# A decode stage with a fourth place for value slices and two buffers for split weights

## What is computed

```python
p = x @ w_in                                    # (560 tokens, 2048) x (2048, 6664)
qa, ka, va, ... = jnp.split(p, ...)
...
k_past = cache_k[l][page_table].reshape(bs, past, H_ATT, HEAD_DIM)
v_past = cache_v[l][page_table].reshape(bs, past, H_ATT, HEAD_DIM)
z = einsum('bqhd,bkhd->bhqk', q, k) * SB_SCALE + bias
log_keep = where(mask, log_sigmoid(-z), 0)
log_pass = cumsum(log_keep, reverse=True) - log_keep
a = where(mask, exp(log_sigmoid(z) + log_pass), 0)
h_att = einsum('bhqk,bkhd->bqhd', a, v)
```

## Time and profile before

| | us |
|---|---|
| median of 3 runs (2784.31 to 2788.75) | 2785.24 |
| the profiled execution's own time | 2780.29 |
| its span in the profile | 2778.6 |
| first stage, from 0 to about | 966 |
| TensorE busy over the span | 2686.6 (97%) |
| DMA moved over the span | 691.84 MB |

### The profile page before, as it was taken

The page is one execution under the profiler, slowest core; times in us unless marked ns, Lnnn a source line. Parts: engine busy times, 40 slices in busy tenths (PEclk is TensorE's granted clock), DMA queues, the critical chain, the costliest instruction groups (busy, mean ns, idle before and its releaser), DMA issues.

```text
span 2778.6 us, 58915 instructions
## 1 busy us (share of the span) xinstructions
PE 2686.6 (97%) x25059; PEld 2545.9 (92%) x25059; DVE 1931.2 (70%) x2366; ACT 1096.1 (39%) x1615; POOL 340.3 (12%) x357
## 2 busy tenths in 40 slices
PE   8999999999999898999999999999998999999998
PEld 7998988888888666799989999999998999999997
DVE  3374555554554287788987787788777888888887
ACT  3221221221221266544645555555653333333331
POOL 3011101111101031111102222222220000000000
PEclk9999999999999999999999999999999999999999
DMA  7889999999999872477537665666678757565732
GB/s 234 297 313 401 407 409 411 411 378 414 407 372 388 304 232 92 112 211 201 157 109 206 192 201 179 199 190 197 186 233 278 236 186 238 160 215 173 233 101 95
DMA packets 542216, 691.84 MB, mean 249 GB/s; under 512 B 25723, under 2 KB 467164, under 8 KB 531538
## 3 DMA queue, kind: packets, MB, share of 16 engines
q1 hardware_dynamic: 465042, 477.59, 52.2%
q0 software_dynamic: 13872, 141.28, 12.5%
q10 hardware_dynamic: 63040, 69.21, 7.3%
HBM read 589.21 MB, written 98.79 MB: 248 GB/s over the span
## 4 chain that ended last, share of the span: by engine, by line
PE 47%; DVE 1%; DMA 1%; SPq 1%; issue 0%; ACT 0%; DVEq 0%; ACTq 0%
PE big_G L2406 15%; PE big_G L2408 15%; PE big_G L2407 15%; DMA raw<-in_w_down 1%; SPq L2261 1%; PE big_G L2515 1%; DMA raw<-in_w_up 0%; PE big_G L2511 0%; PE big_G L2513 0%; PE big_G L2512 0%; DVE raw L2695 0%; DVE wl L2683 0%; DVE base L2695 0%; SPq L2277 0%; DVE big_xl L2703 0%
## 5 line engine op out<-in xcount | busy, mean ns | idle before, releaser
L472 PE MATMUL prj_G<-prj_xh,prj_wh 128*128 128x280 f32 (+1 forms) x1696 | 502.4, 296 | 4.4 <-ACT prj_stage L612 3.2
L474 PE MATMUL prj_G<-prj_xh,prj_wl 128*128 128x280 f32 (+1 forms) x1696 | 496.6, 293 | 0.0
L473 PE MATMUL prj_G<-prj_xl,prj_wh 128*128 128x280 f32 (+1 forms) x1696 | 495.6, 292 | 0.0
L727 DVE STREAM_TRANSPOSE prj_kT<-base 128x4096 f32<-128x4096 f32 x64 | 284.4, 4444 | 259.7 <-PE prj_S L505 259.7
L2544 ACT ACTIVATE wh<-raw 128x768 fp32r<-128x768 f32 (+1 forms) x294 | 279.6, 951 | 374.8 <-PE big_G L2408 200.3
L2683 DVE TENSOR_TENSOR wl<-raw,wh 128x768 fp32r<-128x768 f32 (+1 forms) x294 | 329.7, 1124 | 121.2 <-ACT wh L2544 121.1
L472 PEld LDWEIGHTS prj_G<-prj_xh,prj_wh 128*128 128x128 f32 x1696 | 322.9, 190 | 29.3 <-issue 26.8
L2406 PE MATMUL big_G<-big_xh,wh 128*128 128x272 f32 x1168 | 338.4, 290 | 3.4 <-ACT base L2547 1.8
L2408 PE MATMUL big_G<-big_xh,wl 128*128 128x272 f32 x1168 | 337.9, 289 | 0.0
L2407 PE MATMUL big_G<-big_xl,wh 128*128 128x272 f32 x1168 | 336.5, 288 | 0.0
L2406 PE MATMUL big_G<-ff_window,wh 128*128 128x272 f32 x1116 | 322.7, 289 | 7.4 <-DVE wl L2683 7.4
(11 more groups left out here) (487 smaller groups left out, 6023.1 us busy)
## 6 DMA issues: line engine op xcount, KB each, us to landing
prj_v_nat<-in_cache_v SPq DMA_DIRECT2D x242, 512.0 KB, 7.9
raw<-in_w_up SPq DMA_DIRECT2D x128, 512.0 KB, 4.4
u_scratch<-base SPq DMA_DIRECT2D x60, 952.0 KB, 6.6
ff_window<-u_scratch SPq DMA_DIRECT2D x70, 816.0 KB, 7.2
prj_raw<-in_w_in ACTq DMA_DIRECT2D x103, 512.0 KB, 16.7
raw<-in_w_down SPq DMA_DIRECT2D x120, 384.0 KB, 4.6
raw<-in_w_out SPq DMA_DIRECT2D x60, 512.0 KB, 4.8
ff_left_over<-in_w_down SPq DMA_DIRECT2D x80, 192.0 KB, 6.4
```

The costliest lines, as they stand in the source:

```text
L472: mm(out, w_hi[:, k, m], xh[:, k0 + k, cols], start=(first and k == 0), stop=False)
L473: mm(out, w_hi[:, k, m], xl[:, k0 + k, cols], start=False, stop=False)
L474: last = mm(out, w_lo[:, k, m], xh[:, k0 + k, cols], start=False, stop=(end and k == nk - 1))
L727: V.transpose(flat(kT[:, :, :, :, :].rearrange("p r h b i -> p r (h b i)")), flat(k_nat[k % 2][:, :, :]))\
```

## The change

The places for value slices become four, and the rotation for the last sequence has six places in place of five. The buffers for the split weights, `wh` and `wl`, become two each in place of three. A place for a slice takes 8 KB of a partition, and so do one `wh` and one `wl` together, so that the memory stays the same.

```diff
-VR, EXTRA = 3, 2
+VR, EXTRA = 4, 2
 
 
 def value_slot(m):
 
-    return m % VR if m < LAST else (VR, VR + 1, 1, 2, 0)[(m - LAST) % (VR + EXTRA)]
+    return m % VR if m < LAST else (VR, VR + 1, 0, 1, 2, 3)[(m - LAST) % (VR + EXTRA)]
...
-    RAW, WH, STAGE = 3, 3, 3
+    RAW, WH, STAGE = 3, 2, 3
```

## The result

The changed kernel takes 2793.13 us in the median of 15 runs (2784.49 to 2799.08), the kernel before 2783.26 us in 15 runs beside them (2775.07 to 2788.75). The ratio is 1.0032, with a 95% interval of 1.0021 to 1.0043: 9.9 us between the medians. The forecast was 2782.3 us and "within 0.2%"; the range held the time, and what happened is close to the rival called Slower (2795.9 us).

A forecast was written before the change was run, and what follows sets the result against it. In the first stage TensorE's projection and the DMA stream end nearly together. Terms of -3.0 (up to chunk 90), +3.5, -6.0 and +2.6 sum to -2.9 us, set against the median 2785.24: 2782.3 us, range 2771 to 2797.

The forecast's parts named there:

- Slower: Rival: weights become late, pauses at chunks 46 and 90 lengthen, nothing gained up to 90; +10.7, 2795.9 us; chance 0.28.
- Value waits before 900 us: TensorE's eight waits for value slices can all go: 9.6 us, plus 1.7 us of lower clock, 11.3 in all.
- The six pauses: At six steps the copy-out stands behind a high part that waits for its buffer: TensorE pauses 1.75 us each, 10.5 us.
- I take five: Of the six pauses of 1.75 us, five were charged: 8.75 us.
- at chunk 90 the weights remain the later wait: Of the six places, chunk 90 was left uncharged, its pause still being ended by late weights.
- Chunk 90: TensorE, 6.0 us ahead, meets a late weight load there; 3.0 us of the lead is kept, bounds 0 and 6.0.
- Of the 6.0 us I keep 3.0 and leave the rest to a longer pause there: At chunk 90, DMA engines bring the bytes 3 us earlier; the rest of TensorE's lead goes into a longer pause.
- Weight loads later, +2.6: Second high part waits for its buffer, so following weight loads go out later: 2.6 us once, bounds 0 and 10.3.
- The last sequence, -6.0: The 5.59 us value wait at 942 and lower clock go, 9.2 us; 3 us of new waits; -6.0 kept.
- No gain on values: Rival: value waits only move and six pauses count in full; +4.5, 2789.7 us; chance 0.10.
- the rotation without effect: Rival: in the last sequence the slice behind the heads stays late, giving back 6.0; 2788.3 us; chance 0.05.
- Later stages: Stages behind the first shift as they are; any move beyond the shift would speak against the sum.

The follow-up runs named there:

- experiment 1: Kernel before with only the split weight buffers cut from three to two: 2796.16 us, ratio 1.0040.
- Experiment 8: Changed kernel with copy-out before the next high part, VectorE's scan before low parts, probabilities and queries before the second high part: 2773.64 us, ratio 0.9975.
- experiment 2: Changed kernel with ScalarE's copy-out put ahead of the next step's high part in the six steps: 2778.51 us, ratio 0.9986.
- experiment 3: Changed kernel with value slices loaded in 2 KB runs instead of 4 KB: 2797.13 us, ratio 1.0033.
- experiment 5: Changed kernel with the fourth value place for the last sequence alone: 2796.35 us, ratio 1.0049; also second profiles of two split buffers alone and the changed kernel.
- experiment 9: Kernel before with copy-out, scan, and probabilities and queries all moved ahead: 2792.95 us, ratio 1.0029.

## Why the prediction was wrong, point by point

- **Value waits before 900 us**: right. 9.6 us in eight waits became none, and no lower clock follows where the one at 563 was. The stretch from 650 moves 412 GB/s with the waits gone. The Trainium skill (DMA: Bandwidth & Descriptors, section Bandwidth) gives the 358 GB/s, by which none of it would come back, as a core's share when both cores of an HBM domain stream, and 425 GB/s as measured with one core alone. The 412 GB/s of this one core lie near the second; the prediction had left the condition out.
- **The six pauses**: right in place, cause and size, 1.82 us against 1.75, at four of the six and in experiment 1 at all six. "I take five" and "at chunk 90 the weights remain the later wait" treated the others apart, and there it went wrong.
- **Chunk 90, and chunk 46 with it**: the step that failed. "Of the 6.0 us I keep 3.0 and leave the rest to a longer pause there" let the load come no later than it did and put it right ahead of the copy-out, as in the earlier trace rows: 3.2 + 3.0 = 6.2 us at 90 and 1.75 at 46. Measured were 10.23 and 7.46, together 9.7 us more; with the forecast's -2.9 this gives +6.8, against +9.0 at the end of the stage. The other 2.2 us are not taken apart in full; among them is the lower clock behind chunks 46 and 50, which the sum did not charge (half of 4.66 and of 3.40 us busy, 4.0 in all), with smaller terms of the other sign. Two things were missed. The load got less of the DMA engines, and it was the one for chunk 90 itself, whose high part belongs to the step before, so that the probabilities, the queries and one more high part, 6 us of ScalarE, stood between it and the copy-out. Experiment 8 takes 5.7 us of it away (8.5 us between landing and copy-out became 2.8), with loads as late as before; experiment 2 shows that the order is where the change lost its time.
- **Weight loads later, +2.6**: they do go out later where it matters. The load of chunk 46 was issued 26.8 us ahead of the first matmul of chunk 45 (28.6 in the kernel before), that of chunk 90 25.3 us ahead of the first of chunk 89 (28.0). The cost did not come as a term of its own; any part of it lies in the two long pauses. The median landing is 19.4 us against 19.7, the slowest 32.7 against 30.0.
- **The last sequence, -6.0**: nearly. The 5.59 us went, 2.98 us came (forecast 3), and the lower clock there covers 3.4 us (963.2 to 966.6, 3.25 busy) instead of 10.2 with 7.25 busy, half of 4.0: -4.6 in all.
- **The rival Slower**: right in sign and in place. Its price (+10.7, measured 9.9) is in part luck: it had nothing gained up to chunk 90, where the value waits did go, and it put the two long pauses too low (3.2 and 6.4 us, measured 7.46 and 10.23). With its mechanism, packets taken in turn, experiment 3 agrees: with value packets half as large the weights landed in 14.5 us in the median instead of 19.4. The Trainium skill (DMA: Bandwidth & Descriptors, section Queues, rings and completion order) says that an engine goes round its queues a packet at a time; the 4.9 us of experiment 3 fit that. That it takes values ahead to make a load late fits only at 90, by experiment 5. It had 0.28 and should have had more than the forecast: the earlier trace rows already showed the weights as the weakest queue, and both parts of the change leaned on it.
- **No gain on values; the rotation without effect**: neither happened.
- **Later stages**: "beyond the shift" they moved by 3.2 us (span less the last value matmul: 1817.2 against 1814.0). That is no effect of the change that the traces could tell: the second profile of the changed kernel has 1815.1, and the thirteen profiles run from 1813.5 to 1822.1.

## What to carry to other kernels

Before a buffer is taken from an engine that works in program order, list all that stands behind the instruction that will now wait, up to the one another engine needs, and add it to the wait: here 1.8 us where only the high part and the copy-out stood in the way, and 6 to 10 us in both profiles of the changed kernel where a sequence began and the weights landed late. When a ring is shrunk to feed another, the order tuned to the old sizes has to be changed with it: the same two sizes cost 0.32% in the old order and gained 0.25% in the new, and the new order with the old sizes lost 0.29%. Where several queues keep the DMA engines full, watch each one's time to land: here the weights, with the smallest packets (1.1 KB), came late in the changed kernel, but values came late when their packets were halved (15.0 us of waits) or when they kept three places (15.2 us and, in experiment 9, 35.2 us).

## What the hardware showed that I had not expected

- The pause of 1.82 us at chunk 50 was followed by 3.4 us at a granted clock of 0.51 with TensorE busy throughout (440.90:444.30), half of which is lost. The pauses at 54, 94 and 98, as long, were not followed by any. In the second profile of the changed kernel those at 50 and 94 were. The sum charged the clock to none of the six.
- The same program on the same data paused 1.82 us at chunk 46 in one execution and 6.51 in another. A single profile does not tell which of two causes a late load has. At this place the length goes with whether the load lands before the next gather of keys is issued (experiment 5).
